# Moving the pooled branch of a four-branch mixer into the stage that projects its inputs

## The reference, cut to what matters

```python
proj = xn @ w_in[l]
u_pool = proj[..., :o1]
qkv_dil = proj[..., o1:o2].reshape(B_, S_, 3, DIL_HEADS, DIL_HEAD_DIM)
qkv_sb = proj[..., o2:o3].reshape(B_, S_, 3, SB_HEADS, SB_HEAD_DIM)
u_s5 = proj[..., o3:]
y_pool = pool_mixer(u_pool, pool_w[l], pool_scale[l])
y_dil = dilated_attention(qkv_dil, rel_bias)
y_sb = stick_breaking_attention(qkv_sb)
y_s5 = s5_mixer(u_s5, s5_a_re[l], ...)
```

```python
mean = (cs[:, 1:, sl] - cs[:, lo, sl]) / cnt[None, :, None]
outs.append(mean - uf[:, :, sl])
...
y = jnp.einsum('bsgc,gcd->bsgd', p, w_grp.astype(jnp.float32)).reshape(B_, S_, POOL_WIDTH)
return (y * scale.astype(jnp.float32)).astype(u.dtype)
```

## Time and profile before

| what | us |
|---|---|
| median of three runs | 3651.38 |
| profiled execution | 3652.57 |
| its span | 3650.8 |
| projection stage, begin to last addition on DVE | 1591 to 2293.0 |
| dilated stage, first DMA to the first DMA behind it | 2298.36 to 2560.67 |
| mean granted clock over the span | 0.955 |

### The profile page before, as it was taken

One profiled execution on the slowest core, in us unless ns is written; L12 is line 12 of the kernel. 1 busy time (PEld: TensorE's weight loads), 2 busy tenths in 40 slices (PEclk: granted clock), 3 DMA queues, 4 the chain that ended last, 5 costly groups with the idle time before them and its releaser, 6 DMA issues. The chain is left out here.

```text
span 3650.8 us, 43830 instructions
## 1 busy us (share of the span) xinstructions
PE 3336.9 (91%) x16295; PEld 2663.9 (73%) x16295; DVE 2105.9 (58%) x3004; ACT 1306.3 (36%) x2270; POOL 1290.4 (35%) x1028
## 2 busy tenths in 40 slices
PE   5699999989899999969999999588889989999998
PEld 3577777776688888747888888375557768888887
DVE  5346664465876767883333333575555465555586
ACT  3523333143433334432223333153652233322344
POOL 4121212112655530145544454260435235544111
PEclk8799999889999999979999999799999999999999
DMA  8621112123233347224555332751025523333552
GB/s 255 221 61 46 51 57 90 49 99 110 70 116 101 101 140 241 75 70 134 115 113 121 116 116 93 203 164 64 31 67 152 167 93 101 98 104 101 199 183 98
DMA packets 357916, 418.46 MB, mean 115 GB/s; under 512 B 29798, under 2 KB 257586, under 8 KB 356282
## 3 DMA queue, kind: packets, MB, share of 16 engines
q1 hardware_dynamic: 350968, 391.84, 34.9%
q0 software_dynamic: 6016, 16.93, 1.9%
q10 hardware_dynamic: 722, 6.89, 0.5%
HBM read 294.06 MB, written 120.88 MB: 114 GB/s over the span
## 5 line engine op out<-in xcount | busy, mean ns | idle before, releaser
L2348 POOL TENSOR_TENSOR up_w_lo<-up_w_sum,up_w_hi 128x512 fp32r<-128x512 f32 x176 | 248.5, 1440 | 326.4 <-ACT up_w_hi L2324 324.5
L3282 POOL TENSOR_TENSOR px_w_lo<-px_w_sum,px_w_hi 128x512 fp32r<-128x512 f32 x140 | 204.8, 1493 | 281.4 <-ACT px_w_hi L3133 281.4
L2348 POOL TENSOR_TENSOR up_w_lo<-up_raw,up_w_hi 128x512 fp32r<-128x512 f32 x132 | 201.4, 1541 | 127.5 <-ACT up_w_hi L2324 127.5
L1924 ACT CAST down_hi<-down_room 128x1024 fp32r<-128x1024 f32 x154 | 161.0, 1051 | 210.7 <-PE ps L2204 137.1
L1928 DVE TENSOR_TENSOR down_lo<-down_room,down_hi 128x1024 fp32r<-128x1024 f32 x154 | 190.0, 1239 | 72.6 <-ACT down_hi L1924 71.4
L2324 ACT CAST up_w_hi<-up_w_sum 128x512 fp32r<-128x512 f32 x176 | 99.7, 614 | 323.5 <-DVE up_w_sum L2337 323.5
L766 PE MATMUL ps<-h_hi,stream_hi 128*128 128x512 f32 (+1 forms) x488 | 184.7, 378 | 24.5 <-POOL stream_lo L741 17.2
L2554 PE MATMUL ps<-h_hi_at,up_w_lo 128*128 128x512 f32 x704 | 191.3, 394 | 15.7 <-POOL up_w_lo L2348 15.7
L2554 PE MATMUL ps<-h_hi_at,up_w_hi 128*128 128x512 f32 x704 | 192.5, 396 | 8.0 <-ACT up_w_hi L2324 8.0
L3133 ACT CAST px_w_hi<-px_w_sum 128x512 fp32r<-128x512 f32 x140 | 79.9, 617 | 310.8 <-DVE px_w_sum L3213 310.8
L2554 PE MATMUL ps<-h_lo_at,up_w_hi 128*128 128x512 f32 x704 | 189.3, 391 | 0.0
(11 more groups left out here) (607 smaller groups left out, 8138.0 us busy)
## 6 DMA issues: line engine op xcount, KB each, us to landing
up_raw<-in_w_up SPq DMA_DIRECT2D x88, 512.0 KB, 4.2
down_room<-hid_kept SPq DMA_DIRECT2D x154, 256.0 KB, 2.9
hid_kept<-up_out SPq DMA_DIRECT2D x44, 512.0 KB, 3.6
down_room<-in_w_down SPq DMA_DIRECT2D x88, 256.0 KB, 4.3
px_raw<-in_w_in SPq DMA_DIRECT2D x38, 512.0 KB, 5.2
proj_kept<-xT SPq DMA_DIRECT2D x34, 512.0 KB, 6.0
px_raw<-in_w_gate SPq DMA_DIRECT2D x32, 512.0 KB, 5.2
gates_kept<-xT SPq DMA_DIRECT2D x32, 512.0 KB, 5.2
```

Source lines behind the costliest of these rows:

```text
L1924: nc.scalar.copy(hi[:, u % R], both(u)).then_inc(hi_made, 1)
L2348: nc.gpsimd.tensor_tensor(w_lo[:, s, :], source(t, i), w_hi[:, s, :].bitcast(F32), ALU.subtract).then_inc(lo_made, 1)
L3282: nc.gpsimd.tensor_tensor(self.w_lo[:, s, :], self.source(t, i), self.w_hi[:, s, :].bitcast(F32), ALU.subtract).then_inc(self.lo_made, 1)
```

## The change

The pooled branch leaves the dilated stage. It is computed in the projection stage, one group at each of the pairs 20, 23, 26 and 29 (`POOL_AT`): at t = at-1 SP loads the group's 0.5 MB of `proj_kept`, in pair `at` DVE makes its sums (`pool_sums`) ahead of `u2`, in pair at+1 PE multiplies behind product 3 into the two banks that products 0 and 1 of that pair have left, in pair at+2 ACT scales the result behind the `p1` copy, and SP stores it to a new DRAM tensor, `pool_kept`. Products 1 and 2 of pair at+2 wait for ACT's two operations before they take the banks. At t = 32 SP loads the first dilated group's queries and keys into the 16 KB that the pooled branch had had in the dilated stage, so that `scores(0)` waits for no load; `pool_kept` (2 MB) is loaded back late in that stage. To make room, the projections' result tiles become full-width, and the store by step one DMA instead of two.

In the S5 core POOL loads the chunk in four parts of eight 64 KB DMAs instead of eight of 256 KB at once; it begins when the second value load has landed (before: the second pooled input). The steps of the dilated stage shrink from 45 to 39, and the tables change: inputs 3, 6, 9, 12; outputs 8, 11, 14, 17; gate rows 21, 24, 27, 30, 32, 34, 36, 38; the last two value turns at 16 and 18 instead of 18 and 20.

```diff
@@ Projections.sp @@
+            for g, at in enumerate(self.POOL_AT):
+                if t == at - 1:
...
+                    sp.dma_start(self.pool_u, self.pool_src[:, g, :]).then_inc(self.pool_loaded, 16)
+                if t == at + 2:
+                    sp.wait_ge(self.pool_out, 2 * g + 2)
+                    sp.dma_start(self.pool_kept[:, g, :], self.pool_sums[1 - self.last_sum[g]]).then_inc(self.pool_stored, 16)
+            if t == self.POOL_AT[-1] + 3:
...
+                sp.dma_start(self.first_qk[0], self.first_qk[1]).then_inc(self.qk_loaded, 16)
@@ Projections, ScalarE, behind the p1 copy @@
             nc.scalar.copy(self.p1[:, :], self.bank(t, 0)).then_inc(self.p1_copied, 1)
+            if t - 2 in self.POOL_AT:
+                g = self.POOL_AT.index(t - 2)
+                act.wait_ge(self.pool_mixed, g + 1)
+                for n in range(2):
+                    nc.scalar.activation(self.pool_sums[1 - self.last_sum[g]][:, n * BANK:(n + 1) * BANK], self.bank(t - 1, n), ACT.Copy,
+                                         scale=self.pool_scale[:, g:g + 1]).then_inc(self.pool_out, 1)
@@ Projections.vector @@
                 for which in range(3):
                     sums_of(t + 1, which)
+            if t in self.POOL_AT:
+                pool_sums(self.POOL_AT.index(t))
@@ Projections.tensor @@
+                if before - 1 in self.POOL_AT and j < 2:
+                    pe.wait_ge(self.pool_out, 2 * self.POOL_AT.index(before - 1) + j + 1)
...
+            if i == 3 and t - 1 in self.POOL_AT:
...
+                for n in range(2):
+                    ins = nc.tensor.matmul(self.bank(t, n), self.pool_w[:, g, :], self.pool_sums[self.last_sum[g]][:, n * BANK:(n + 1) * BANK], start=True, stop=True)
+                ins.then_inc(self.pool_mixed, 1)
@@ dilated @@
-    core = S5Core(c, io, s5, rooms, yT, (3, 7, 11, 15), (9, 13, 17, 21), (25, 28, 31, 34, 37, 40, 42, 44), u_loaded[1])
+    core = S5Core(c, io, s5, rooms, yT, (3, 6, 9, 12), (8, 11, 14, 17), (21, 24, 27, 30, 32, 34, 36, 38), v_loaded[1])
...
-            if b == 0:
+            if n and b == 0:
                 pe.wait_ge(qk_loaded[n], 16)
@@ S5Core, POOL @@
+        def load_chunk(m):
+            for s in range(S5_L):
+                pool.dma_start(self.rooms.chunk[s * SC:(s + 1) * SC, 8 * m:8 * m + 8, :],
+                               self.s5["u"].rearrange("g ch s k -> s ch g k")[s, :, 8 * m:8 * m + 8, :]).then_inc(self.in_loaded[m], 16)
...
-        for step in range(S5_L):
-            pool.dma_start(self.rooms.chunk[step * SC:(step + 1) * SC, :, :], self.s5["u"].rearrange("g ch s k -> s ch g k")[step]).then_inc(self.in_loaded[0], 16)
+        load_chunk(0)
         load_inputs(pool, self.s5, self.rooms, 0, self.in_loaded[0])
...
+        load_chunk(1)
...
             make_state(m)
             if m < 2:
+                load_chunk(m + 2)
```

More of the change, by code:

```diff
@@ L2877, in second_block @@
         raw = c.nc.alloc_sbuf_tensor_at("mg_raw", [P, 2, BANK], F32, offset=MERGE_AT["raw"])
-        pool_and_dilated(c, io, proj, skewed, s5, rooms, heads, yT, xT, ident)
+        dilated(c, io, proj, skewed, pool_kept, s5, rooms, heads, yT, xT, ident)
         c.end_stage()
@@ L3025, in __init__ @@
         for t, pair in enumerate(pairs):
-            totals[t % 2] += sum(32 if kind == "steps" else 16 for _, kind, _ in pair)
+            totals[t % 2] += 16 * len(pair)
             self.stored_by.append(totals[t % 2])
@@ L3080, in store @@
                 if kind == "steps":
-                    for half in range(2):
-                        k = S5_N // 2
-                        sp.dma_start(dst[:, :, half * k:(half + 1) * k],
-                                     self.by_step(part)[:, half, :].rearrange("p (s k) -> p s k", s=S5_L)).then_inc(self.stored[t % 2], 16)
+                    sp.dma_start(dst, self.by_step(part)).then_inc(self.stored[t % 2], 16)
                 else:
@@ L3152, in post @@
                     act.wait_ge(self.stored[(t - 1) % 2], self.stored_by[t - 1])
-                act.wait_ge(self.x_stored, 16)
-                for half in range(2):
-                    last = nc.scalar.copy(self.by_step(part)[:, half, :].rearrange("p (s k) -> p s k", s=S5_L),
-                                          view[:, half, :].rearrange("p (k s) -> p s k", s=S5_L))
-                last.then_inc(self.posted, 1)
+                nc.scalar.copy(self.by_step(part), view.rearrange("p h n -> p (h n)").rearrange("p (k s) -> p s k", s=S5_L)).then_inc(self.posted, 1)
         H = self.H
@@ L3355, in _, with dilated @@
             px.tensor(pe)
-def pool_and_dilated(c, io, proj, skewed, s5, rooms, heads, yT, spare, ident):
+def dilated(c, io, proj, skewed, pool_kept, s5, rooms, heads, yT, spare, ident):
     nc = c.nc
-    G, BLOCKS = len(POOLS), 3 * NB
+    BLOCKS = 3 * NB
     ROW = DH * DE + DH
@@ L3448, in side_pe @@
     def side_pe(pe):
-        for s in range(N_POOL):
-            g = s - 1
-            if 0 <= g < G:
-                if g == 0:
-                    pe.wait_ge(pool_loaded, 32)
-                pe.wait_ge(p_ready, g + 1)
-                if g >= 2:
-                    pe.wait_ge(p_out, g - 1)
-                for n in range(2):
-                    last = nc.tensor.matmul(c.ps[:, S0 + 2 * (g % 2) + n, :], wg[:, g, :], pooled[:, g % 2, n * BANK:(n + 1) * BANK],
-                                            start=True, stop=True)
-                last.then_inc(p_mixed, 1)
-            yield
         def scores(j):
@@ L3721, in side_sp @@
         load_bias(2)
-        load_values(9)
+        for j in range(6, 8):
+            load_values(j)
         sp.wait_ge(done, 1)
@@ L3747, in _ @@
         def _(pe):
-            own = core.pe(pe)
-            for step, _ in enumerate(side_pe(pe)):
+            own, side = core.pe(pe), side_pe(pe)
+            for step in range(N_DIL + N_MIX):
                 turn_values(pe, step)
+                next(side)
                 next(own, None)
@@ L3756, in _ @@
         def _(dve):
-            own = core.dve(dve)
-            for step, _ in enumerate(side_dve(dve)):
+            own, side = core.dve(dve), side_dve(dve)
+            for step in range(N_DIL + N_MIX):
                 take_values(dve, 0, step)
+                next(side)
                 next(own, None)
@@ L3765, in _ @@
         def _(act):
-            own = core.act(act)
-            for step, _ in enumerate(side_act(act)):
+            own, side = core.act(act), side_act(act)
+            for step in range(N_DIL + N_MIX):
                 take_values(act, 1, step)
+                next(side)
                 next(own, None)
```

156 lines of the change are left out of this document (83 added, 73 removed).

## The result

The changed kernel takes 3674.95 us, median of four runs (3670.61 to 3676.02), against 3649.95 us of the kernel before (3648.41 to 3652.16; a fourth run joins the three named at the start): a ratio of 1.0066, 95% interval 1.0048 to 1.0083. Forecast were 3647.5 us and a range up to 3659. Repeated beside other kernels it took 3669.93 us against 3653.46, ratio 1.0046 (1.0030 to 1.0061); the table of experiments gives ratios, since the medians of before differ by up to 3.6 us from one batch of runs to another.

What follows compares the result with a forecast made beforehand. It took the projection stage as bound by PE alone, the dilated stage by loads, then the S5 chain, then gate rows. +16.1 - 12.0 - 8.0 = -3.9 us turned the median 3651.38 into 3647.5 us, range 3636 to 3659.

Steps and rivals of the forecast that it cites:

- The start of the dilated stage: Dilated stage's start: fewer loads in front, first S5 input earlier, first state at 2343 against 2352.54 before, 44.6 us in.
- one of my signs of being wrong: Dilated stage's start: the prediction would be wrong if the first S5 state waits for a DMA.
- The projection stage: Projection stage: eight added matmuls on PE, 7.3 us, and four new waits for ACT, 8.8 us; together +16.1 us.
- PE feels nothing: Projection stage: DVE's pooled sums, about 7.1 us for w = 16, make `a` at worst 2.5 us late, costing PE nothing.
- Rival 3: Projection stage: the four new waits cost PE its clock, +16 us more, net +12, 3663 us; chance 0.08.
- The chain behind it: Dilated stage's S5 rounds after the first state: outputs 5.1, then 7.8 us, rounds of 26.1; gate rows gain 12.0 us.
- Rival 5: Dilated stage: POOL's small DMAs do not overlap, parts 2 and 3 stand in the chain, +20, net +16, 3667; chance 0.02.
- The gain of 12.0 us: Dilated stage: the first gate row comes at 2454.9 instead of 2466.93, from the earlier start and the S5 chain.
- The gate rows begin 17.9 us later as before: Dilated stage: from the end of the last S5 outputs to the first gate row, 17.9 us, unchanged.
- The tail: Dilated stage from first gate row to end: two gate units beside six steps, six alone, 85.8 against 93.8 us, gain 8.0.

## Why the prediction was wrong

Forecast and profiled execution lie some 28 us apart in the two stages: 3 at the border, 10 more at the end of the last outputs, 7 more on the way to the first gate row, and 8 in the tail.

**The start of the dilated stage: the number right, partly by luck.** First S5 input at 26.2 us (forecast 23 to 32), first state at 45.2 (44.6). But DVE was not busy all the way, as I had reckoned:

```profile
2347.74 0.69 DVE L3498 COPY yT<-ps 128x512 f32<-128x512 f32 x1 [5.29 <-PE ps L3487]
```

It began 8.8 us into the stage (forecast 11.6) and then stood idle 5.29 us behind PE's S5 input, which itself waited 3.83 us for a load. The early begin paid for a wait that I had left out, and one of my signs of being wrong, a first state that waits for a DMA, did show.

**The projection stage: mechanism right, size off by 3.6 us.** Four matmul pairs cost 7.7 us (7.3), ACT's waits 4 x 1.83 = 7.3 (8.8). "PE feels nothing" of DVE's sums failed: they took 10.4 us for w = 16, not 7.1 (see the last section), and PE waited 0.36, 0.61 and 0.93 us, 1.9 in all. Rival 3's mechanism came once in four, some 1.6 us behind the fourth wait (rows at 2237 to 2240). These sum to 18.5 of the 19.7.

**The chain behind it: the step that failed.** I let the first outputs run at full clock, took 7.8 us for the other three, and let each round else be the last one of before (23.4); before's own first round took 31.6. The first round came to 31.7 us instead of 25.7: outputs at half clock (+4.2), begun 1.5 us later behind the state. The third came to 30.3 instead of 26.1: the fourth input stood 5.92 us for loads that POOL had issued behind a chunk part, which I had priced at nothing, and outputs took 9.3. Rival 5 is not what happened: the part's eight issues took POOL 4.2 us. The second, at 23.9, was as in before. In the repetition all outputs were slow, no input but the first waited for loads, and the rounds came to 33.7, 27.3 and 27.3, so that the fourth state stood 132.7 us into the stage (131.2 here): an output at full speed gains little while POOL's loads for the next input are late. The gain of 12.0 us at the first gate row was 9.0 at the first state, 2.1 at the end of the last outputs, and a loss of 5.0 at the first gate row.

**"The gate rows begin 17.9 us later as before": failed by 7.2 us.** I did not read what stands ahead of the last gelu in ACT's and PE's lists, nor what SP moves beside the last reload. The last outputs now stand at step 17 of the blocks (in before at step 21, which is step 15 of the blocks behind six pooled ones), and there a longer stretch of PE's block work and a logarithm come ahead of the gelu (4.1 us), and SP's store and load fall beside the reload (3.1 us, read from rows and not tested).

**The tail: failed by 7.6 us.** I took a step beside gate units at before's 5.2 us. They took 6.3 (37.9 us for six steps and two units), with PE at its lower level for part of it: 6.49 us for the first half unit, 5.15 in before. The six units alone took 55.5, as forecast (56.0).

The gains of the single edits do not add up, and no run makes the chain reach a round of 24 us in all its rounds in the shortened stage with whole outputs: whether a PE that comes neither early nor late can be had there at all stays open, and so does what puts an output at the lower level. Shown is that the output's length is on the chain, that it is 5.1 to 9.3 us by the granted clock, and that full speed bought with other PE work, useful or not, brought the outputs later by about as much or more.

## What to carry to other kernels

Work that is taken out of a stage with a chain through an in-order engine was also what filled that engine's time until the chain needed it: count what the engine then waits for, and price the next link at either clock, since here the wait just ahead of it did not tell which it would be. When steps are renumbered, read for every link what now stands ahead of it in each engine's list, on the engines that are far from busy too. A wait that a moved step puts on a full engine is priced from the reader's list; moving the reader's instruction into its own idle time gave back some 10 us here for nothing.

## What the runs showed of the hardware

DVE was slower beside POOL's arithmetic. In the dilated stage of before, with POOL only issuing DMAs, a shifted addition of 128x1022 took 1.22 us and a copy of 128x2 0.18:

```profile
2310.67 0.18 DVE L3537 COPY xT<-xT 128x2 f32<-128x2 f32 x1
2310.89 1.22 DVE L3538 TENSOR_TENSOR xT<-xT 128x1022 f32<-128x1022 f32 x1
```

In after, where POOL's weight subtractions run at that time (5.17 us for three from 2205.66 on, in the fourth group), the same took

```profile
L3266 DVE TENSOR_TENSOR xT<-xT 128x1022 f32<-128x1022 f32 x3 | 6.8, 2268 | 0.1
L3266 DVE TENSOR_TENSOR xT<-xT 128x1023 f32<-128x1023 f32 x4 | 4.9, 1224 | 0.1
L3265 DVE COPY xT<-xT 128x2 f32<-128x2 f32 x3 | 3.4, 1143 | 0.1
```

(the mean in ns is behind the busy time), about 1.0 us more for three operations in a row of each group (in the groups of w = 4, 8 and 16 the first and the last of these lines and an operation on 128x4), and not for the addition of 128x1023, which began before POOL did. The Trainium skill, SBUF — State Buffer, section SBUF: two separate sides, has a port pair that a DVE operation with two SBUF inputs or in a 2-port mode and a GpSimd operation take in turn, each for a whole instruction, while the other stands still. The rows agree: each stretched operation is longer by most of one POOL subtraction (1.3 us), whatever its own size.
